# Layer-1 modulation columns moved into the recurrent stage, row sums spread over both feed-forward halves, and earlier skew DMAs

## The reference

```python
m_lat = (silu_c @ w_mod[l] + b_mod[l]).reshape(Bsz, N_MOD, 1, D)     # w_mod[l]: 1024 x 9216, nine vectors
m_ctx = (silu_cc @ w_mod[l] + b_mod[l]).reshape(N_MOD, D)
x = x + 0.5 * m_lat[:, 2] * swiglu(modulate(rms_norm(x), m_lat[:, 0], m_lat[:, 1]), ffn_in[l, 0], ffn_out[l, 0])
h_lat = modulate(rms_norm(x), m_lat[:, 3], m_lat[:, 4])
# mixer of layer 0: attention and a recurrence (rwkv); of layer 1: window attention
x = x + m_lat[:, 5] * o_lat
x = x + 0.5 * m_lat[:, 8] * swiglu(modulate(rms_norm(x), m_lat[:, 6], m_lat[:, 7]), ffn_in[l, 1], ffn_out[l, 1])
# second block: six vectors a layer from w_ada (1024 x 6144), a mixer with three branches, a conv feed-forward
```

## Time and profile before

| what | value |
|---|---|
| three runs | 3791.85, 3799.59, 3799.35 us; median 3799.35 us |
| profiled execution | 3791.85 us, span 3790.0 us |
| TensorE busy | 3543.5 us (93%) |
| VectorE busy | 2157.8 us (57%) |
| ScalarE busy | 1416.4 us (37%) |
| DMA | 453.90 MB, mean 120 GB/s |

### The profile page before, as it was taken

The page is one execution under the profiler, slowest core; times in us unless marked ns, Lnnn a source line. Parts: engine busy times, 40 slices in busy tenths (PEclk is TensorE's granted clock), DMA queues, the critical chain, the costliest instruction groups (busy, mean ns, idle before and its releaser), DMA issues.

```text
span 3790.0 us, 61710 instructions
## 1 busy us (share of the span) xinstructions
PE 3543.5 (93%) x26870; PEld 2969.8 (78%) x26870; DVE 2157.8 (57%) x3440; ACT 1416.4 (37%) x2310; POOL 145.1 (4%) x258
## 2 busy tenths in 40 slices
PE   6999999888799999999987999999999999999898
PEld 4887885778778878877875998767887778879898
DVE  3765445777756763567466554653464443566675
ACT  3222334444332222322245543443242332445553
POOL 0110000000000100010100000020000000010000
PEclk8999998899999999999998999999999999999999
DMA  6664120000025652465624552221224552223453
GB/s 221 210 196 138 52 91 28 3 3 3 3 78 178 200 161 95 162 217 187 137 96 154 158 186 82 67 73 61 89 89 167 179 176 100 82 91 129 153 182 112
DMA packets 268413, 453.90 MB, mean 120 GB/s; under 512 B 15376, under 2 KB 158864, under 8 KB 262896
## 3 DMA queue, kind: packets, MB, share of 16 engines
q1 hardware_dynamic: 241296, 357.79, 28.8%
q0 software_dynamic: 26848, 92.17, 8.2%
HBM read 447.24 MB, written 1.94 MB: 119 GB/s over the span
## 4 chain that ended last, share of the span: by engine, by line
PE 76%; DVE 14%; DMA 5%; ACT 4%; issue 2%; SPq 0%; DVEq 0%; ACTq 0%
PE bank L1129 75%; DVE W L1957 4%; DVE W L1948 3%; DVE WR L1948 2%; ACT W L1603 2%; ACT WR L1603 1%; DMA ring<-in_w_ada 1%; PE bank L1374 1%; DMA ring<-in_w_up 1%; DMA ring<-in_w_mod 1%; DVE H L1948 1%; DVE HL L1948 1%; DMA ring<-in_ffn_out 1%; DVE small L2265 0%; ACT H L1603 0%
## 5 line engine op out<-in xcount | busy, mean ns | idle before, releaser
L1129 PE MATMUL bank<-HH,WR 128*128 128x512 f32 (+1 forms) x9312 | 2440.2, 349 | 79.1 <-DVE WR L1948 49.2
L1129 PEld LDWEIGHTS bank<-HH,WR 128*128 128x128 f32 x9312 | 1648.2, 193 | 333.8 <-DVE WR L1948 62.7
L1129 PE MATMUL bank<-HL,WR 128*128 128x512 f32 (+1 forms) x4656 | 1606.1, 345 | 0.0
L1948 DVE TENSOR_TENSOR WR<-ring,WR 128x2048 fp32r<-128x2048 f32 (+3 forms) x300 | 673.4, 2249 | 533.6 <-ACT WR L1603 533.0
L1129 PEld LDWEIGHTS bank<-HL,WR 128*128 128x128 f32 x4656 | 898.6, 193 | 96.9
L1603 ACT ACTIVATE WR<-ring 128x2048 fp32r<-128x2048 f32 (+3 forms) x300 | 561.8, 1879 | 820.3 <-PE bank L1129 621.6
L1603 ACT ACTIVATE W<-bank 64x256 f32<-64x256 f32 (+3 forms) x676 | 294.0, 444 | 789.1 <-PE bank L1129 745.0
L1129 PE MATMUL bank<-W 64*64 64x64 f32 (+5 forms) x6304 | 351.6, 249 | 50.0 <-ACT W L1603 29.1
L1957 DVE SCALAR_TENSOR_TENSOR W<-ring,vec,W 128x1024 f32<-128x1024 f32 x252 | 311.6, 1280 | 89.6 <-DMA ring<-in_w_mod 66.0
L1129 PEld LDWEIGHTS bank<-W 64*64 64x64 f32 (+3 forms) x6304 | 266.1, 141 | 121.6 <-ACT W L1603 48.9
L1957 DVE SCALAR_TENSOR_TENSOR W<-bank,vec,W 128x510 f32<-128x510 f32 (+1 forms) x206 | 130.5, 634 | 186.5 <-ACT W L1603 182.9
(11 more groups left out here) (114 smaller groups left out, 2215.0 us busy)
## 6 DMA issues: line engine op xcount, KB each, us to landing
ring<-in_ffn_in SPq DMA_DIRECT2D x176, 512.0 KB, 5.1
ring<-in_w_mod POOLq DMA_DIRECT2D x128, 512.0 KB, 4.5
ring<-in_w_in SPq DMA_DIRECT2D x52, 1024.0 KB, 5.1
ring<-in_ffn_out SPq DMA_DIRECT2D x176, 256.0 KB, 3.6
ring<-in_w_up SPq DMA_DIRECT2D x88, 512.0 KB, 5.0
ring<-in_w_ada SPq DMA_DIRECT2D x32, 1024.0 KB, 5.7
ring<-in_w_down SPq DMA_DIRECT2D x88, 256.0 KB, 3.5
ring<-in_w_ada POOLq DMA_DIRECT2D x32, 512.0 KB, 4.6
```

Of the source, the lines that this page charges most:

```text
L1129: return e.matmul(o, l, r, start=start, stop=stop, skip_group_check=True)
L1948: put(e.tensor_tensor(o, a, b, op), *events)
```

## The change

Vectors 6, 7 and 8 of m1 are made by columns (blocks 3 and 4: eight slabs, then four with two pieces of 1024 columns) in `rwkv`, behind rounds 2, 6, 25, 26 and 27 of its chunks: fourteen steps in forty places. In order they fall at chunk 0 rounds 6 and 27, chunk 1 round 25, chunk 2 rounds 2 and 26, chunk 3 rounds 6 and 27, chunk 4 round 6, then a transpose at 27, chunk 5 round 25, chunk 6 rounds 2 and 26, chunk 7 round 2, and the second transpose at 26. MROW lies in the ring slot of the lora weights there. Each of "f00", "2" and "f10" now makes one vector in its output half at rate 0.9, and keeps the row slot until its end. The input halves run at rate 0.55 with five, five and four vectors (one of f10's is latent only). The skew DMAs go to the input half of "2", at its fifth `between`.

```diff
@@ -550,7 +550,7 @@
             "m0": (A["w_mod"][0], 9216, "b_mod0", "cc", PLAN9, 0), "m1": (A["w_mod"][1], 9216, "b_mod1", "cc", PLAN9, 1),
             "a0": (A["w_ada"][0], 6144, "b_ada0", "cc2", {1: "g_mix0", 4: "g_ffn0"}, 0),
             "a1": (A["w_ada"][1], 6144, "b_ada1", "cc2", {1: "g_mix1", 4: "g_ffn1"}, 1)}
-        PREVIOUS = {"a0": ("m0", 0)}
+        PREVIOUS = {"a0": ("m1", 4)}
         PENDING = []
 
         def columns(t, blocks):
@@ -562,7 +562,7 @@
             for b in blocks:
                 nc_ = min(2048, n - 2048 * b)
                 ks = 2048 // nc_
-                MROW[t, b] = wv(24576 + 512 * (b % 2), [512])
+                MROW[t, b] = hold.get("mrow", [wv(24576 + 512 * i, [512]) for i in range(2)])[b % 2]
                 for k in range(0, KD, ks):
                     s = slab([(w[P * k:P * (k + ks), 2048 * b:2048 * b + nc_], 0, 0)], ks, nc_, "raw")
                     ORDER.append(("mod_mm", t, b, k, ks, nc_ // 512, s))
@@ -589,8 +589,8 @@
             ORDER.extend(steps_)
             del steps_[:]
 
-        def background(gen, rate, late=0):
-            tick = [-rate * late]
+        def background(gen, rate):
+            tick = [0.0]
 
             def step():
                 tick[0] += rate
@@ -599,7 +599,7 @@
                     next(gen, None)
             return step
 
-        def ffn(name, w_in, w_out, i0, ntok, mod, after, bg=None, rows=None, deep=None):
+        def ffn(name, w_in, w_out, i0, ntok, mod, after, bg=None, rows=None):
             modnorm("n" + name, ntok, mod, i0, i0 + 1)
             groups = [[g * 256, g * 256 + P, FF + g * 256, FF + g * 256 + P] for g in range(11)]
             if rows:
@@ -612,11 +612,10 @@
                 for _ in rows[0]:
                     pass
                 now(PENDING)
-            if rows and not deep:
-                rows_end()
-            lin_deep(name + "o", w_out, G, ntok, mod, i0 + 2, after, name + "i", each=background(*deep) if deep else None)
-            if deep:
-                for _ in deep[0]:
+            lin_deep(name + "o", w_out, G, ntok, mod, i0 + 2, after, name + "i",
+                     each=background(rows[2], rows[3]) if rows else None)
+            if rows:
+                for _ in rows[2]:
                     pass
                 rows_end()
 
@@ -665,7 +664,7 @@
                     v_ready=(DVES, ("vt", "ev", 3))))
             return units
 
-        def even_mixer():
+        def even_mixer(mods0, mods1):
             wi = A["even_w_in"][0]
             ORDER.append(("inputs_rest",))
             modnorm("ne", NT, 0, 3, 4)
@@ -713,8 +712,9 @@
                     lora.append(("k_dir", (n - 2) // 4, (n - 2) % 4))
             lora.append(("lora_g",))
             hold["keep"] = SLABS[s]["ring"]
-            woven(lora, att)
-            rwkv(s)
+            woven(lora, att, taken(lambda: list(mods0)))
+            hold["mrow"] = [slot(s)[:, i, :] for i in range(2)]
+            rwkv(s, mods1)
             release()
             out = taken(lambda: lin("eout", "add", A["even_w_out"][0], chunks(0, 8), KD, NT, ready="eo", mod=0, idx=5, norm="n2"))
             a, b, c = readout()
@@ -768,20 +768,30 @@
         WKV_OFF = [[256 + 64 * c for c in range(4)] + [64 * c for c in range(4)],
                    [256 + 64 * c for c in (3, 2, 1, 0)] + [64 * c for c in (3, 2, 1, 0)]]
         ROUNDS = 29
+        WKV_MODS = (2, 6, 25, 26, 27)
         PZ = [[small[:, 8 * d + 4 * a:8 * d + 4 * a + 4] for a in range(2)] for d in range(2)]
 
-        def rwkv(s):
+        def rwkv(s, mods1):
             tiles = [H[:, k, :] for k in range(4)] + [F[:, 12, :], F[:, 13, :], slot(s)[:, 3, :], wv(11776, [512])]
             tiles += [wv(512 * i, [512]) for i in range(8)] + [wv(24576 + 512 * i, [512]) for i in range(7)]
             for n in ("al be ka rho pi alt bet kat vt n nt aak n2 n2t jd arb ark w1t w2 S U to").split():
                 T[n] = Tile(tiles.pop(0))
             barrier()
             ORDER.append(("wkv_start",))
+            mods = taken(lambda: list(mods1))
+            share = len(mods) / 41
             ORDER.extend(("wkv", d) for d in range(2))
+            done = 0
             for c in range(8):
                 for r in range(1, ROUNDS + 1):
                     ORDER.extend(("wkv", d) for d in range(2))
+                    if r in WKV_MODS:
+                        upto = round(share * (5 * c + WKV_MODS.index(r) + 1 + c // 7))
+                        ORDER.extend(mods[done:upto])
+                        done = upto
+            ORDER.extend(mods[done:])
             hold["slot"], hold["keep"] = hold["keep"], None
+            del hold["mrow"]
             barrier()
 
         def readout():
@@ -1008,7 +1018,11 @@
                 ORDER.append(("gain", name, k, dst, gain))
             barrier()
 
-        cols = {"m0": columns("m0", [0]), "a0": columns("a0", [2]), "a1": columns("a1", [0, 1, 2])}
+        def skewed():
+            ORDER.append(("skew",))
+            yield
+
+        cols = {"m0": columns("m0", [0]), "m1": columns("m1", [3, 4]), "a0": columns("a0", [2]), "a1": columns("a1", [0, 1, 2])}
         ORDER.append(("begin",))
         next(cols["m0"])
         ORDER.append(("warm",))
@@ -1034,14 +1048,12 @@
         ORDER.append(("split_next",))
         pairs_of = lambda t, a, b, nv=2: [(t, idx, nv) for idx in range(a, b)]
         ffn("f00", A["ffn_in"][0, 0], A["ffn_out"][0, 0], 0, NT, 0, "ne",
-            rows=(row_sums(pairs_of("m0", 2, 8), 1), 0.6))
-        even_mixer()
-        ffn("2", A["ffn_in"][0, 1], A["ffn_out"][0, 1], 6, NT, 0, "nf10",
-            rows=(row_sums(pairs_of("m0", 8, 9) + pairs_of("m1", 0, 5), 1), 0.6))
+            rows=(row_sums(pairs_of("m0", 2, 7), 0), 0.55, row_sums(pairs_of("m0", 7, 8), 0), 0.9))
+        even_mixer(cols["m0"], cols["m1"])
+        ffn("2", A["ffn_in"][0, 1], A["ffn_out"][0, 1], 6, NT, 0, "nf10", (skewed(), 0.2),
+            rows=(row_sums(pairs_of("m0", 8, 9) + pairs_of("m1", 0, 4), 0), 0.55, row_sums(pairs_of("m1", 4, 5), 0), 0.9))
         ffn("f10", A["ffn_in"][1, 0], A["ffn_out"][1, 0], 0, NT, 1, "no",
-            rows=(row_sums(pairs_of("m1", 5, 9, 1) + pairs_of("a0", 0, 3), 0), 0.74),
-            deep=(row_sums(pairs_of("a0", 3, 4), 0), 0.2, 24))
-        ORDER.append(("skew",))
+            rows=(row_sums(pairs_of("m1", 5, 6, 1) + pairs_of("a0", 0, 3), 1), 0.55, row_sums(pairs_of("a0", 3, 4), 0), 0.9))
         odd_mixer(cols["a0"])
         ffn("11", A["ffn_in"][1, 1], A["ffn_out"][1, 1], 6, 256, 1, "fin", (context2(), 1.0))
         for l in range(2):
```

## The result

The changed kernel takes 3830.19 us (median of four runs, 3823.48 to 3835.46), the kernel before 3795.6 us (four runs, 3790.75 to 3799.59): a ratio of 1.0091, 95% interval 1.0073 to 1.0108. It is slower, outside the range of the forecast (3777 to 3818) and on the side that was given 0.30. The profiled execution has a span of 3822.7 us, 32.7 us more than before.

A forecast was written before the change was run, and what follows sets the result against it. TensorE, busy 3543.5 of 3790.0 us, was taken as the bound. Terms -24.0 - 12.9 - 4 + 4.5 + 21 + 14 = -1.4 us gave 3798 us against the median, 8-in-10 range 3777 to 3818.

The forecast's parts named there:

- Tail stalls: Ends of the input halves of "f00" and "2": waits for VectorE's last row accumulations shrink, -24.0 us together.
- f10: Input half of "f10": fewer row steps, sums and transposes, and no waits on VectorE's split, -12.9 us.
- Deep halves: Three output halves: eight row steps at rate 0.9 make the fourth slab's split slightly late, 1.5 us each, +4.5.
- the split of the third slab comes first: Output halves: VectorE does the third slab's split before the row steps, so is free some 5.8 us after the start.
- the deep halves stall: Rival, output halves: row landings of 6 us cost 4 us each and some half clock, +9, 3807 us; chance 0.08.
- Skew, new place: Input half of "2": a row slab queues behind the skew on POOL, TensorE stands 15 to 18 us; +21.
- the skew is cheap: Rival, input half of "2": the stall shrinks to under 3 us, -18, 3780 us; chance 0.25.
- Weight slabs are not late: Input half of "2": SP's slabs move on beside the skew, so no slab stall is added to the 21 us.
- Skew, old place: Behind "f10": removing the sixteen skew DMAs there ends late landings and a slower norm, -4 us.
- rwkv: Column work in rwkv: 10 us for products and transposes, 4 for the kept PSUM bank, +14; bounds 4 and 31.
- Loads are covered: rwkv: column loads cost nothing, with DMA share 0.01 and one slab per 25 us.
- rwkv pays in full: Rival, rwkv: no slabs hidden, bank costs 2.5 us a chunk; 17.5 + 13 instead of 14, 3814 us; chance 0.22.

The follow-up runs named there:

- e1: The changed kernel with the sixteen skew DMAs back at their old place behind "f10": 3799.38 us, ratio 1.0026 against the kernel before.
- e5: The changed kernel with the row steps of all three output halves at rate 0.2 instead of 0.9: 3789.87 us, ratio 1.0018 against the kernel before.
- e2: The changed kernel with row slabs in the output halves no longer holding back a later weight slab's split: 3807.42 us, ratio 1.0059 against the kernel before.
- e9: The changed kernel with all fourteen column steps in rwkv placed behind round 2, one or two a chunk: ratio 1.0096 against the kernel before.
- e8: The changed kernel with output halves at rate 0.2, skew DMAs at the start of rwkv, rows instead of rwkv columns: 3769.01 us, ratio 0.9953.
- e11: The changed kernel, rwkv columns kept, with output halves at rate 0.2 and skew DMAs at the start of rwkv: 3777.65 us, ratio 0.9981.
- e3: The changed kernel without columns in rwkv, those vectors being row sums in f10's input half at rate 0.74: 3820.25 us, ratio 1.0094.
- e12: e10 with the skew DMAs behind "f10" instead of at the start of rwkv: 3756.11 us, ratio 0.9915 against the kernel before.
- e10: e8 with the row sums spread, input halves of "2" and "f10" at rate 0.66: 3765.70 us, ratio 0.9945 against the kernel before.
- e6: The changed kernel without the products of ten of twelve rwkv column slabs, bank and loads kept: ratio 1.0086 against the kernel before.

## Why the forecast was wrong

- **Tail stalls** (forecast -24.0): right. The input halves give -10.5 and, in e1, -11.0; another 3.1 and 3.5 us appear in the output halves of e5, where before had 5.3 and 6.2 us at half clock, behind the stalls of the earlier trace rows, and e5 has none. Together -28.
- **f10** (-12.9): right, -13.7.
- **Deep halves** (+4.5): this is the step that failed, "I take 1.5 each". It measured 8.5 + 8.2 + 7.4 = +24.1. The sentence it stood on, "the split of the third slab comes first", is not what the planner does: even the second slab's split stands behind five row steps. With it made true (e2) the halves still cost 3.9 + 3.0 + 1.2. So the order is worth 16.0 of e5's 34.9 us, and seven steps in one slab the other 18.9. The rival "the deep halves stall", with a chance of 0.08, had the place but another cause: it blamed slow row landings and put them at 4 us each. The stalls were 9.1 to 10.0 us, and in the first of them VectorE waited 3.3 us for landings.
- **Skew, new place** (+21): right in the queue's part, 24.4 in size, but with an error of a slab in the rest. In the time of the kernel before (the stage begins 16.4 us later now) the skew began at 1195.2, not at 1198.3; the sixteenth issue came 36.1 us later (38.6 forecast), and the row landed 8.7 us after its issue, at 1240.8 (forecast 1244 to 1247). The split was done 8.6 us after that (9 forecast), and TensorE went on at 1249.4, 4 to 7 us before the 1253 to 1256 of the forecast. But it had run out of slabs at 1226.8 and not at 1237.7, since it had 3B and 4A and not 4B. So it stood 22.57 us, not 15 to 18: two errors of 10.9 and 4 to 7 us went opposite ways, and that the sum came out near 21 is in part luck. That a stall came at all is no luck; the rival that the skew is cheap is out. A link was missed too: "Weight slabs are not late". ScalarE waited 19.75 us for 4B's landing and began its split at 1246.30 of the changed kernel's time, when TensorE had stood since 1243.18; with 1.91 and 2.29 us for the two parts of a split it would have gone on at 1250.5 at best. So SP's slabs do move on beside the skew, as the rule from the Trainium skill that stood there has it ("DMA: Bandwidth & Descriptors", "Queues, rings and completion order": the engines take the queues in turn), but late enough for a stall of 7 us of their own, which the rows' 22.57 covers.
- **Skew, old place** (-4): at most 2.
- **rwkv** (+14): 17.5 to 21.0 in five profiles, with -1.4 behind it. In seven chunks it is 12.2 without a kept bank (10 forecast for the products of eight) and 6.5 more with it (4 forecast, bounds 0 and 13). "Loads are covered" failed in part: no product waited for its slab, but waits of 5.8 to 7.2 us without a releaser came with the loads. That is mis-sized, and nearer the forecast than the rival "rwkv pays in full", which had 30.5: a chunk grew by 2.7 us, less than the 3 that were to decide for the rival. What the forecast says of round 2, that it hides a slab, nearly holds for the slabs of block 3: 0.2 us each in e9, some 0.5 with the clock taken into account. How the rest divides between the bank, block 4, the loads and the clock stays open.
- The last sum, which now stands in the next norm's first group, had been put at 0. From "f00" to the attention it is 1.3 us more in every kernel that has it there.

The forecast's sum of -1.4 misses +32.7 by 34. By the stages it is about 20 in the output halves, 6 in rwkv and behind it, 5 in the "rest", where the skew's old place was to give 4 and nothing shows, 3 by the skew's new place, and 2.5 in the tails, since part of their gain lies hidden in the output halves; the small terms cancel. The range was too narrow because the worst case of the deep halves, "with slower landings 4", was bounded by one row's landing and not by what happens if VectorE's list has another order. The same rule of the planner was missed twice: in the skew it was worth 10.9 us, most of which other errors made up.

## What to carry to other kernels

Where the order of an engine is made by a planner, run its rule by hand at the place that the change touches, before costing anything: here one condition put five row steps ahead of a split. Background work cost nothing here when each piece was followed by the urgent work in time, and it stalled TensorE when seven pieces stood in a row; so pace it, and don't bunch it even where the engine is half idle. And put bursts of small DMAs where neither a load on the same queue nor a stage of short matmuls waits behind them: the same sixteen cost 24 us in "2", 3 to 10 in rwkv and at most 2 behind "f10".

## What was not expected of the hardware

**Late instructions.** In a stage of short matmuls TensorE stood 8.11 us in e8 and 7.0 in e11 while sixteen DMAs of 124-byte runs filled the DMA engines, and started again behind a 16 KB packet of the instruction queue. It is not the skew alone: smaller waits of this kind, up to 1.8 us each, stand in rwkv of every kernel that loads columns there. In rwkv of all profiles each such wait of 0.2 us or more ends 1.1 to 1.7 us after the end of a 16 KB packet of that queue, and before, e3 and e12, which have neither columns nor skew there, have none. The Trainium skill, "Runtime: NRT & Kernel Launch", section "Instruction fetch mechanics", says that an engine's instructions are refilled in 16 KiB blocks over a DMA queue and that a block's border is mostly hidden. The trace agrees with the block; that it is hidden fails here by 8.11 us. That TensorE waited for its instructions, and they behind the packets of the skew or of a column slab, is the likeliest reading; whose instructions a packet holds, and when it was asked for, the traces don't show.

**The same stage at another clock.** The attention has the same instructions in all profiles, and took 128.1 to 129.1 us in six of them, with 27 to 31 us at half clock, 133.8 to 134.1 in five (41 us at half clock) and 136.7 to 137.0 in three (48 to 57 us). Two windows of the same 54 us, before and e3:

```profile
616.00:670.00 54.00, 45.51 (x204) 21.83 (x204) 30.83 (x80) 28.44 (x68) 0.00 (x0) 0.78 0.01 3
```

```profile
616.00:670.00 54.00, 52.01 (x163) 24.22 (x162) 24.89 (x63) 23.46 (x54) 0.00 (x0) 0.53 0.00 0
```

The clock was 0.78 and 0.53. With nothing changed in that stage, 8 us come and go, as much as the bound of 0.2%; a stage table tells such a shift from an effect, a total doesn't. It may not be chance alone: all five kernels with rate 0.2 in the output halves (e5, e8, e10, e11, e12) are among the longer ones, with 4.7 to 7.6 us more than before, against three of the other nine (e2, e3, e6). Why they would be is open, with one profile each.

**The sixteenth DMA.** POOL's last skew issue came 26.63 us behind the others before, 24.13 after, and 17.13 (e8), 18.74 (e10) and 21.47 (e11) in rwkv, with no releaser named. Why sixteen and not fifteen stays open.
